# One evacuation put later on ScalarE, one row sum put earlier on VectorE, in a two-block transformer kernel

## The chip, the cores and the metric

The kernel runs on one core of a Trainium2 chip. The metric is the device time of one execution in microseconds (us). The median of three runs before the change is 1176.83 us (1176.0 to 1178.22). The core's engines are named as in the profile: PE is TensorE (PEld its weight loads), DVE is VectorE, ACT is ScalarE, POOL is GpSimd, and SP is SyncE, which issues most DMAs. Each engine runs its own instructions strictly in the order in which they were written; semaphores order the engines among each other.

## The reference, cut to what matters

```python
def project(h, w_in, w_dec_up, b_dec):            # first block; h is 256 x 1024, once for x and once for ctx
    z = h @ w_in
    q, k, v, g, dd, cb, cc, ch, ga, gb = jnp.split(z, ...)
    zd = dd @ w_dec_up + b_dec
    log_a = jax.nn.log_sigmoid(zd) / DECAY_TAU     # decays of the gated linear attention, both directions
...
mod_lat = jnp.split(jax.nn.silu(c) @ w_ada + b_ada, 6)   # shifts, scales and gates, a vector of 6 * 1024
pl = project(modulate(rmsnorm(x, g_mix), sh1, sc1), ...)
pc = project(modulate(rmsnorm(ctx, g_mix), sh1c, sc1c), ...)
o_l = gla_bidir(...)                               # attention over x, from the states that ctx leaves
mix_l = merge_branches(o_l, g, cb, cc, ch, ga, gb, ...)  # y_gla and y_conv, gated, merged, projected
x = x + gt1 * mix_l
x = x + gt2 * swiglu(modulate(rmsnorm(x, g_ffn), sh2, sc2), w_ffn_in, w_ffn_out)
return second_block(rmsnorm(x, g_final), ...)      # feed forward, attention, feed forward
```

## The kernel before, in words

Everything is float32. A product is made of three passes: each weight and each activation is held as a rounded high part (`whi`, `A_hi`, `B_hi`) and the remainder (`wlo`, `A_lo`, `B_lo`), and PE does high by high, high by low and low by high.

The first block's projections are cut into 45 **units** (the list `P1`), each 256 columns wide: unit 0 is `dd`, 1 and 2 are `k`, 3 to 6 are `v`, 7 and 8 are `q`, 9 to 20 are `cb`, `cc`, `ch` four times over, 21 to 24 are `g`, 25 to 28 `conv_out`, and so on. `U_K` is 1, `U_V` is 3, `U_Q` is 7, `U_CB` is 9. A unit's weights come by one DMA of 1 MB into one of three `raw` buffers, ACT writes `whi` (the first half of `split(u)`), DVE subtracts to get `wlo` (the second half, which also gives the buffer free for the load of unit u + 3), and PE runs the unit. The units `k` and `v` are computed for `x` and for `ctx` and take two banks of PSUM each: unit 2 has banks 4 and 7, unit 3 banks 5 and 6, unit 4 banks 4 and 7, unit 5 banks 5 and 6. All later units have one bank, 4 and 5 by turns. Before it starts unit u, PE waits until its `lo_ready` has come and until the unit that last held its banks has been **evacuated** (`wait_banks`): for `v` ACT does this with two copies, for `ch` DVE does it with a multiplication by `cc` (two units later PE uses that bank again).

ACT and DVE each walk through the same loop over u. In its round u, ACT evacuates unit u - 1 (`evac1(u - 1)`), does its half of `split(u + 2)`, and then what the attention needs at that point (`gla_front`, `gla_step`), the `ch` convolution's middle tap (`conv_tap`) and its high part. The exceptions stand at the start: at u = `U_K + 1` unit 2 is evacuated inside `gla_front`, between the exponentials `decays(0)`, `decays(1)` and the part `log_decays(2)`; at u = `U_V` unit 3 is evacuated inside `gla_front` ahead of `decays(2)` and `decays(3)`. The `decays(g)` wait for DVE's running sums of the decays, `sums(g)` (semaphores `scan_done` and `d_done`).

`decays(2)` and `decays(3)` have to be done before DVE can form the decayed keys (`decayed_keys`), which PE turns after half of unit 6 (`turn_keys`).

The modulation vector of `w_ada` is made beside the units, 256 columns at a time (numbers 0 to 15 in this part). POOL issues the 1 MB load of number n into the one buffer `ada_raw` when number n - 1 is through (`load_ada`). DVE's `adapt(n)` waits for the landing and folds the eight 128 x 256 pieces into a row of sums, eight instructions one after the other. The table `MOD_STEP` says at the end of which round u DVE does which `adapt(n)`.

At u = 21 DVE's round is: evacuate unit 20 (`ch`, the fourth), `split(23)`, `conv(3)` with four taps and a product, `adapt(8)`. At u = 20 it has only `split(22)`.

Of the kernel before, what the change touches and what calls it, by code (L numbers as in the profile page):

```python
# [54 lines left out]
U_K, U_V, U_Q, U_CB = (P1.index((s, 0)) for s in ("k", "v", "q", "cb"))  # L55
# [62 lines left out]
ADA_LAST = ADA_P2 + NADA2  # L118


MOD_STEP = {4: 0, 5: 1, 7: 2, 9: 3, 11: 4, 13: 5, 16: 6, 18: 7, 21: 8, 24: 9, 26: 10, 28: 11, 30: 12, 32: 13, 34: 14, 36: 15}

ADA_FFN = [n for n in range(len(ADA)) if NADA1 <= n < ADA_P2 or n >= ADA_LAST]
ADA_MIX = [n for n in range(len(ADA)) if n not in ADA_FFN]
ADA_DVE = [n for n in range(len(ADA)) if n in MOD_STEP.values() or n in ADA_FFN or ADA_P2 <= n < ADA_P2 + 4]
ADA_POOL = [n for n in range(len(ADA)) if n not in ADA_DVE]
# [22 lines left out]
def build(nc, a, out):  # L149
    with ExitStack() as ctx:  # L150
# [711 lines left out]
        def _(act):  # L862
# [7 lines left out]
            def run(o, i, f=ACT.Copy, **kw):  # L870
                return nc.scalar.activation(o, i, f, **kw)  # L871

            def split(u, i=0, count=1):

                if isinstance(i, int) and u + 3 * i >= UNITS:
                    return
                act.wait_ge(landed[ring(u)], landings(u, i))
                if not isinstance(i, int) or u + 3 * i >= RING:
                    act.wait_ge(unit_used, lin(3, i, u - RING + 1))
                run(whi[ring(u)][:], raw[ring(u)][:]).then_inc(hi_ready, count)  # L880
# [66 lines left out]
            def conv_high(n):  # L947
                act.wait_ge(v_done, n + 1)
                run(B_hi[:, 2 * n:2 * n + 2, :], uS.rearrange("p (m t) -> p m t", m=2)).then_inc(vhi_done, 1)

            def evac1(u):
                kind, n = P1[u]
                eng, count = EV1[u]
                b = BANKS1[u]
                act.wait_ge(unit_used, u + 1)
                two = slice(2 * n, 2 * n + 2)
                b3 = [bank[x][:].rearrange("p (m t) -> p m t", m=2) for x in b]
                if kind == "dd":
                    run(dd_out, bank[0][:, 0:P]).then_inc(act_evac, 1)
                elif kind == "k":  # L960
                    run(kT1[:, two, :], b3[0])
                    run(kTc[:, two, :], b3[1]).then_inc(act_evac, 1)
                elif kind == "v":
                    run(v_l[:, :, UC * n:UC * n + UC], b3[0])
                    run(v_c[:, :, UC * n:UC * n + UC], b3[1]).then_inc(act_evac, 1)
                elif kind == "q":
                    run(qT1[:, two, :], b3[0], scale=float(HK) ** -0.5).then_inc(act_evac, 1)
                elif kind in ("cb", "cc"):
                    if n >= 2:
                        act.wait_ge(v_done, n - 1)  # L970
                    run((cbS if kind == "cb" else ccS)[n % 2], bank[b[0]][:]).then_inc(act_evac, 1)
                elif kind == "conv_out":
                    run(yT[:, two, :], b3[0]).then_inc(act_evac, 1)
                elif kind == "g":
                    if n:
                        act.wait_ge(dve_evac, EV1[u - 1][1])
                    run(T0, bank[b[0]][:], ACT.Sigmoid).then_inc(sig_done, 1)
                elif kind in ("ga", "gb"):
                    run((siga if kind == "ga" else sigb)[:, two, :], b3[0], ACT.Sigmoid).then_inc(act_evac, 1)
                    if kind == "ga":  # L980
                        act.wait_ge(ont_tr, n + 1)
                        run(B_hi[:, two, :], bank[6 + n % 2][:].rearrange("p (m t) -> p m t", m=2))\
                            .then_inc(onhi_done, 1)
                elif kind == "gla_out":
                    act.wait_ge(mg_done, n + 1)
                    run(A_hi[:, two, :], (T0, T1)[n % 2].rearrange("p (m t) -> p m t", m=2)).then_inc(mghi_done, 1)

            def conv_tap(n):

                act.wait_ge(dve_evac, EV1[P1.index(("ch", n))][1])  # L990
                for m in range(2):
                    c = VEC["w_conv"] + KD + 2 * n + m
                    ins = run(yS[:, T * m:T * m + T], uS[:, T * m:T * m + T], scale=vec[:, c:c + 1])
                ins.then_inc(tap_done, 1)

            def log_decays(g0):

                act.wait_ge(zd_mm, 2 * g0 + 4)
                for s in range(2):
                    for g in (g0, g0 + 1):  # L1000
                        d, p, order = gla_pass(g)
                        E = pair3(Eb[g] if s == 0 else Lb[g])
                        for h in range(2):
                            col = VEC["b_dec"] + H1 * d + 2 * p + h
                            ins = run(token_halves(E[:, h, :]), decay_part(g, s, h), ACT.Abs, bias=vec[:, col:col + 1])
                        ins.then_inc(z_abs, 1)

            def soft_part(g):

                act.wait_ge(z_abs, 2 * g + 4)  # L1010
                for v in (Eb[g], Lb[g], Eb[g + 1], Lb[g + 1]):
                    ins = run(v, v, ACT.Exp, scale=-1.0)
                link(ins)
                for v in (Eb[g], Lb[g], Eb[g + 1], Lb[g + 1]):
                    run(v, v, ACT.Ln, bias=1.0).then_inc(z_log, 1)

            def decays(g):

                d = g // 2
                act.wait_ge(scan_done, g + 1)  # L1020
                R, E = pair3(Mc[g % 2]), pair3(Eb[g])
                lo, hi = slice(0, T - 1), slice(1, T)
                run(E[:, :, lo] if d == 0 else E[:, :, hi], R[:, :, hi] if d == 0 else R[:, :, lo], ACT.Exp,
                    scale=1.0 / 16).then_inc(ex_done, 1)
                act.wait_ge(d_done, g + 1)
                run(alpha[:, g], alpha[:, g], ACT.Exp, scale=1.0 / 16)
                run(Qb[g], Ml[g % 2], ACT.Exp, scale=1.0 / 16)
                run(Lb[g], Ml[g % 2], ACT.Exp, scale=-1.0 / 16).then_inc(eq_done, 1)

            def key_tokens(g):  # L1030

                act.wait_ge(kt_tr, g + 1)
                run(k_tok[g].rearrange("p a b c -> p (a b c)"), bank[g][:]).then_inc(kt_sb, 1)

            def ctx_key_tokens(g):

                act.wait_ge(ktc_tr, g + 1)
                run(Eb[g], bank[g][:]).then_inc(ktc_sb, 1)
# [12 lines left out]
            def gla_front(u):  # L1051

                if u == U_K:
                    log_decays(0)
                    soft_part(0)
                if u == U_K + 1:
                    decays(0)
                    decays(1)
                    evac1(U_K + 1)
                    log_decays(2)  # L1060
                    soft_part(2)
                if u == U_V:
                    evac1(U_V)
                    decays(2)
                    decays(3)
                if u == U_V + 3:
                    for g in range(4):
                        ctx_key_tokens(g)
                if u == U_Q:
                    for g in range(4):  # L1070
                        key_tokens(g)

            def gla_step(slot):

                if slot in (2, 3, 4):
                    scale_state(0, slot - 2)
                    scale_state(1, slot - 2)
                if slot in (9, 10, 11):
                    scale_state(2, slot - 9)
                    scale_state(3, slot - 9)  # L1080
# [175 lines left out]
            split(2)  # L1256

            for u in range(N1):
                if u and u not in (U_V, U_V + 1):
                    evac1(u - 1)  # L1260
                if u:
                    split(u + 2)
                gla_front(u)
                gla_step(2 * (u - 1 - U_Q) + 1)
                if P1[u - 1][0] == "ch":
                    conv_tap(P1[u - 1][1])
                if P1[u - 2][0] == "ch":
                    conv_high(P1[u - 2][1])
                gla_step(2 * (u - U_Q))
                if u == U_CB + 7:  # L1270
                    head_squares()
# [621 lines left out]
        def _(dve):  # L1893
# [626 lines left out]
            for u in range(N1):  # L2520
# [14 lines left out]
                if u == U_CB + 8:  # L2535
                    norm_heads()
                if u in MOD_STEP:
                    n = MOD_STEP[u]
                    adapt(n, 0, acc[:, UC * ada_pos(n):UC * ada_pos(n) + UC], ADA[n][0])
# [60 lines left out]
```

## Time and profile before

| | |
|---|---|
| median of the runs | 1176.83 us |
| the profiled execution's own time | 1176.83 us |
| its span in the profile | 1174.9 us |
| PE busy, DVE busy, ACT busy | 96%, 73%, 48% of the span |
| mean granted clock of PE | 0.978 of full speed |

The span is counted from the first to the last instruction that the profile shows; the profiled execution's own time is 1.9 us more. PE's busy time is modelled at the ends of matmuls, so a busy PE is not one at its peak; what can be read safely is when a matmul starts and how long PE sat idle before it. A row of the timeline gives the start, the duration of the merged group, the engine, the line, the operation and its tiles, the count, and in brackets the idle time before it with what ended it. Almost all instructions of one engine stand on the line of a helper, so tiles and times tell which one it is.

### The profile page before, as it was taken

How to read it: one execution, taken by the hardware profiler on the slowest of the kernel's cores; microseconds unless marked ns; L12 is line 12 of the kernel's file. 1: busy time of each engine (PE TensorE's matmuls, PEld its weight loads, DVE VectorE, ACT ScalarE, POOL GpSimd, SP SyncE). 2: the span in 40 equal slices, each digit the busy share in tenths (PEclk: the TensorE clock that was granted, in tenths of full speed). 3: DMA queues.
4: the chain of work that ended last, by engine and by line, in shares of the span. 5: the costliest groups of instructions: out<-in, count | busy, mean ns of one | idle time of the engine just before them, and what ended most of it. 6: DMA issues, size and time to landing. Idle time of an engine off the chain costs nothing.

```text
span 1174.9 us, 19118 instructions
## 1 busy us (share of the span) xinstructions
PE 1130.0 (96%) x7764; PEld 1025.0 (87%) x7764; DVE 857.3 (73%) x1072; ACT 569.7 (48%) x729; POOL 146.4 (12%) x162
## 2 busy tenths in 40 slices
PE   2999999999999999999899999999999989999996
PEld 2999988999999888888788888899989989888885
DVE  2678766897877787787877887778655796755676
ACT  3595433544433544444545444455655536444442
POOL 4000000100001000000200000020476561000000
PEclk8999999999999999999899999989999989999999
DMA  9924654688866487787468877647744745655770
GB/s 288 310 84 144 208 163 139 200 285 278 289 203 211 164 272 250 261 265 272 160 198 272 263 238 252 224 145 260 251 147 153 238 144 170 227 195 181 234 246 36
DMA packets 192548, 250.28 MB, mean 213 GB/s; under 512 B 4860, under 2 KB 171967, under 8 KB 192351
## 3 DMA queue, kind: packets, MB, share of 16 engines
q1 hardware_dynamic: 183838, 216.92, 56.7%
q0 software_dynamic: 8640, 32.38, 8.2%
q8 instruction: 51, 0.84, 0.3%
q14 instruction: 19, 0.15, 0.0%
HBM read 248.23 MB, written 1.05 MB: 212 GB/s over the span
## 4 chain that ended last, share of the span: by engine, by line
PE 87%; DVE 7%; issue 2%; SPq 2%; ACT 1%; DMA 1%; POOL 0%; POOLq 0%; DVEq 0%; ACTq 0%
PE twin L1296 84%; DVE wlo L1902 2%; DVE arena L1910 2%; DVE arena L1902 2%; PE twin L1357 1%; DMA arena<-in_w_ada 1%; ACT arena L871 1%; ACT whi L871 0%; DVE X L1902 0%; PE twin L1622 0%; SPq L564 0%; SPq L514 0%; PE twin L1739 0%; PE twin L1410 0%; DVE B_lo L1902 0%
## 5 line engine op out<-in xcount | busy, mean ns | idle before, releaser
L1296 PE MATMUL twin<-A_both,whi 128*128 128x256 f32 (+1 forms) x2208 | 579.9, 339 | 1.2 <-DVE arena L1902 1.1
L1902 DVE TENSOR_TENSOR wlo<-raw,whi 128x2048 fp32r<-128x2048 f32 x169 | 397.4, 2352 | 121.3 <-ACT whi L871 121.2
L1296 PE MATMUL twin<-A_both,wlo 128*128 128x256 f32 x1632 | 436.7, 280 | 0.0
L871 ACT ACTIVATE whi<-raw 128x2048 fp32r<-128x2048 f32 x169 | 323.1, 1912 | 207.8 <-PE twin L1296 206.6
L1296 PEld LDWEIGHTS twin<-A_both,whi 128*128 128x128 f32 x2208 | 371.5, 190 | 43.6 <-issue 6.2
L1296 PEld LDWEIGHTS twin<-A_both,wlo 128*128 128x128 f32 x1632 | 309.8, 190 | 11.1 <-DVE A_both L1902 0.2
L1910 DVE SCALAR_TENSOR_TENSOR arena<-ada_raw,arena 128x256 f32<-128x256 f32 (+1 forms) x308 | 149.4, 485 | 11.0
L871 ACT ACTIVATE arena<-twin 128x512 f32<-128x512 f32 (+5 forms) x167 | 88.5, 555 | 114.9 <-PE twin L1296 85.5
L871 ACT ACTIVATE arena<-arena 128x512 f32<-128x512 f32 (+7 forms) x132 | 69.8, 558 | 150.1 <-DVE arena L1902 114.4
L1296 PE MATMUL twin<-whi,B_hi 128*128 128x512 f32 (+2 forms) x340 | 126.6, 372 | 0.2 <-DVE B_lo L1902 0.2
L1296 PE MATMUL twin<-wlo,B_hi 128*128 128x512 f32 (+2 forms) x340 | 125.1, 368 | 0.0
L1296 PE MATMUL twin<-whi,B_lo 128*128 128x512 f32 (+2 forms) x340 | 125.1, 368 | 0.0
L1296 PE MATMUL twin<-whi,A_both 128*128 128x256 f32 x640 | 118.8, 288 | 4.6 <-DVE A_both L1902 4.6
L1902 DVE TENSOR_TENSOR arena<-arena,twin 128x512 f32<-128x512 f32 x92 | 62.6, 685 | 64.4 <-ACT arena L871 50.1
L1296 PEld LDWEIGHTS twin<-whi,A_both 128*128 128x128 f32 x640 | 101.5, 195 | 5.9 <-issue 5.8
L1296 PE MATMUL twin<-wlo,A_both 128*128 128x256 f32 x320 | 91.3, 285 | 0.0
L1296 PE MATMUL twin<-arena 128*128 128x1 f32 (+10 forms) x656 | 80.9, 296 | 0.1
L1296 PEld LDWEIGHTS twin<-whi,B_lo 128*128 128x128 f32 x340 | 64.1, 189 | 11.3 <-issue 0.7
L1296 PEld LDWEIGHTS twin<-wlo,B_hi 128*128 128x128 f32 x340 | 64.1, 188 | 10.7
L1296 PEld LDWEIGHTS twin<-arena 128*128 128x128 f32 (+5 forms) x656 | 66.6, 174 | 7.8 <-DVE arena L2225 0.3
L1296 PEld LDWEIGHTS twin<-whi,B_hi 128*128 128x128 f32 x340 | 64.1, 189 | 10.2 <-issue 1.1
L1296 PE MATMUL twin<-B_hi,whi 128*128 128x256 f32 x224 | 63.9, 285 | 1.9 <-DVE B_lo L1902 1.1
(134 smaller groups left out, 986.4 us busy)
## 6 DMA issues: line engine op xcount, KB each, us to landing
raw<-in_w_in SPq DMA_DIRECT2D x48, 1024.0 KB, 5.7
raw<-in_ffn_w_in SPq DMA_DIRECT2D x44, 1024.0 KB, 5.1
ada_raw<-in_w_ada POOLq DMA_DIRECT2D x28, 1024.0 KB, 6.5
ada_raw<-in_w_ada SPq DMA_DIRECT2D x24, 1024.0 KB, 5.4
raw<-in_w_ffn_in SPq DMA_DIRECT2D x22, 1024.0 KB, 5.1
raw<-in_ffn_w_out SPq DMA_DIRECT2D x22, 1024.0 KB, 4.9
raw<-in_w_ffn_out SPq DMA_DIRECT2D x11, 1024.0 KB, 5.1
arena<-in_w_ada SPq DMA_DIRECT2D x8, 1024.0 KB, 11.8
```

The lines of the kernel that those rows point to most:

```text
L871: return nc.scalar.activation(o, i, f, **kw)
L1296: return nc.tensor.matmul(o, l, r, start=start, stop=stop, **kw)
L1357: ins = nc.tensor.transpose(bank[norm_bank(n, b)][:, c:c + P], src[:, t, P * k:P * k + P], ident)
L1902: return nc.vector.tensor_tensor(o, x, y, op)
L1910: return nc.vector.scalar_tensor_tensor(out=o, in0=x, scalar=sc, in1=y, op0=op0, op1=op1)
```

## The change

Two things move; nothing is added or taken away.

```diff
-MOD_STEP = {4: 0, 5: 1, 7: 2, 9: 3, 11: 4, 13: 5, 16: 6, 18: 7, 21: 8, 24: 9, ...}
+MOD_STEP = {4: 0, 5: 1, 7: 2, 9: 3, 11: 4, 13: 5, 16: 6, 18: 7, 20: 8, 24: 9, ...}
...
                 if u == U_V:
-                    evac1(U_V)
                     decays(2)
                     decays(3)
...
             for u in range(N1):
-                if u and u not in (U_V, U_V + 1):
+                if u and u != U_K + 2:
                     evac1(u - 1)
```

`U_K + 2` is 3, the same round as `U_V`, so in round 3 nothing is different but the evacuation that was taken out of `gla_front`. In round 4 the ordinary `evac1(3)` now runs.

ACT, rounds 3 and 4 of the loop, before. The copies from `twin2` and `twin3` are an evacuation (banks 5 and 6, then 4 and 7), `whi2<-raw2` is `split(5)`, `whi0<-raw0` is `split(6)`, the rows that wait for `scan_done` begin `decays(2)` and `decays(3)`.

```order
L871 ACTIVATE whi2<-raw2 128x2048 [waits unit_used,landed2]
L871 ACTIVATE arena<-twin2 128x2x256 [waits unit_used]
L871 ACTIVATE arena<-twin3 128x2x256
L871 ACT_TABLE_LOAD
L871 ACTIVATE arena<-arena 128x2x255 [waits scan_done]
L871 ACTIVATE arena<-arena 128x8 [waits d_done]
L871 ACTIVATE arena<-arena 128x512 x2
L871 ACTIVATE arena<-arena 128x2x255 [waits scan_done]
L871 ACTIVATE arena<-arena 128x8 [waits d_done]
L871 ACTIVATE arena<-arena 128x512 x2
L871 ACTIVATE whi0<-raw0 128x2048 [waits unit_used,landed0]
```

The same stretch of ACT in the changed kernel:

```order
L871 ACTIVATE whi2<-raw2 128x2048 [waits unit_used,landed2]
L871 ACT_TABLE_LOAD
L871 ACTIVATE arena<-arena 128x2x255 [waits scan_done]
L871 ACTIVATE arena<-arena 128x8 [waits d_done]
L871 ACTIVATE arena<-arena 128x512 x2
L871 ACTIVATE arena<-arena 128x2x255 [waits scan_done]
L871 ACTIVATE arena<-arena 128x8 [waits d_done]
L871 ACTIVATE arena<-arena 128x512 x2
L871 ACTIVATE arena<-twin2 128x2x256 [waits unit_used]
L871 ACTIVATE arena<-twin3 128x2x256
L871 ACTIVATE whi0<-raw0 128x2048 [waits unit_used,landed0]
```

The two copies of unit 3 have moved from ahead of eight instructions of the decays, four of which wait for DVE, to behind them.

DVE, rounds 20 and 21, before. `wlo1` is `split(22)`, `X<-arena,twin2` is the evacuation of unit 20, `wlo2` is `split(23)`, the rows on `X` are `conv(3)`, the two rows on `ada_raw` are `adapt(8)`, and the last one begins the evacuation of unit 21.

```order
L1902 TENSOR_TENSOR wlo1<-raw1,whi1 128x2048 [waits hi_ready]
L1902 TENSOR_TENSOR X<-arena,twin2 128x512 [waits vlo_done,act_evac,unit_used]
L1902 TENSOR_TENSOR wlo2<-raw2,whi2 128x2048 [waits hi_ready]
L1910 SCALAR_TENSOR_TENSOR X<-X,arena 128x4x63 [waits tap_done]
L1910 SCALAR_TENSOR_TENSOR X<-X,arena 128x4x63
L1910 SCALAR_TENSOR_TENSOR X<-X,arena 128x4x63 [waits dve_chain]
L1910 SCALAR_TENSOR_TENSOR X<-X,arena 128x4x63
L1902 TENSOR_TENSOR X<-arena,X 128x512 [waits dve_chain]
L1906 TENSOR_SCALAR arena<-ada_raw,arena 128x256 [waits ada_landed_p]
L1910 SCALAR_TENSOR_TENSOR arena<-ada_raw,arena 128x256 [waits ada_mac] x7
L1902 TENSOR_TENSOR arena<-arena,twin2 128x512 [waits sig_done]
```

The same stretch of DVE in the changed kernel (its line numbers are one lower):

```order
L1901 TENSOR_TENSOR wlo1<-raw1,whi1 128x2048 [waits hi_ready]
L1905 TENSOR_SCALAR arena<-ada_raw,arena 128x256 [waits ada_landed_p]
L1909 SCALAR_TENSOR_TENSOR arena<-ada_raw,arena 128x256 [waits ada_mac] x7
L1901 TENSOR_TENSOR X<-arena,twin2 128x512 [waits vlo_done,act_evac,unit_used]
L1901 TENSOR_TENSOR wlo2<-raw2,whi2 128x2048 [waits hi_ready]
L1909 SCALAR_TENSOR_TENSOR X<-X,arena 128x4x63 [waits tap_done]
L1909 SCALAR_TENSOR_TENSOR X<-X,arena 128x4x63
L1909 SCALAR_TENSOR_TENSOR X<-X,arena 128x4x63 [waits dve_chain]
L1909 SCALAR_TENSOR_TENSOR X<-X,arena 128x4x63
L1901 TENSOR_TENSOR X<-arena,X 128x512 [waits dve_chain]
L1901 TENSOR_TENSOR arena<-arena,twin2 128x512 [waits sig_done]
```

The eight instructions of `adapt(8)`, the first of which waits for a DMA, have moved from behind the evacuation of unit 20, `split(23)` and `conv(3)` to ahead of them. PE, POOL and SP have the same instructions in the same order as before.

## Rows read from the trace of the kernel before

**Rows 1.** The page: busy time of PE over the span.
```profile
PE 1130.0 (96%) x7764; PEld 1025.0 (87%) x7764; DVE 857.3 (73%) x1072; ACT 569.7 (48%) x729; POOL 146.4 (12%) x162
```

**Rows 2.** The page: chain that ended last, shares of the span by engine.
```profile
PE 87%; DVE 7%; issue 2%; SPq 2%; ACT 1%; DMA 1%; POOL 0%; POOLq 0%; DVEq 0%; ACTq 0%
```

**Rows 3.** Busy time by stretches: us, busy PE, PEld, DVE, ACT, POOL, PEclk, DMA.
```profile
91.00:97.00 6.00, 6.00 (x52) 6.00 (x51) 5.90 (x14) 3.16 (x5) 0.00 (x0) 1.00 0.56 172
```

**Rows 4.** Timeline of PE: the first matmuls of units 4 and 5.
```profile
79.24 0.40 PE L1296 MATMUL twin<-whi,A_both 128*128 128x256 f32 x2
...
90.76 0.40 PE L1296 MATMUL twin<-whi,A_both 128*128 128x256 f32 x2
```

**Rows 5.** Timeline of ACT, 84 to 98 us: evacuation, decays, `split(6)`.
```profile
85.81 1.06 ACT L871 ACTIVATE arena<-twin 128x512 f32<-128x512 f32 x2
...
91.63 0.63 ACT L871 ACTIVATE arena<-arena 128x510 f32<-128x510 f32 x1 [1.68 <-DVE arena L2158]
94.47 1.25 ACT L871 ACTIVATE arena<-arena 128x8 f32<-128x8 f32 x3 [2.21 <-DVE arena L1902]
95.63 1.90 ACT L871 ACTIVATE whi<-raw 128x2048 fp32r<-128x2048 f32 x1
```

**Rows 6.** Timelines: DVE's last decayed key; PE's first turning of keys.
```profile
98.84 0.68 DVE L1902 TENSOR_TENSOR arena<-arena 128x512 f32<-128x512 f32 x1
...
108.04 1.91 PE L1410 MATMUL twin<-arena 128*128 128x128 f32 x16
```

**Rows 7.** PE around its longest idle time in a run of units.
```profile
947.09 0.77 PE L1296 MATMUL twin<-whi,A_both 128*128 128x256 f32 x2 [4.56 <-DVE A_both L1902]
...
951.57 0.40 PE L1296 MATMUL twin<-whi,A_both 128*128 128x256 f32 x2
```

**Rows 8.** Busy time by stretches, around the same place.
```profile
944.50:947.00 2.50, 0.00 (x0) 0.00 (x0) 2.50 (x3) 0.00 (x0) 2.20 (x2) 0.51 0.02 5
...
949.00:951.00 2.00, 2.00 (x11) 2.00 (x11) 1.87 (x4) 1.36 (x3) 0.00 (x0) 0.50 1.14 365
```

**Rows 9.** Timeline of PE around two shorter idle times.
```profile
878.77 0.63 PE L1622 MATMUL twin<-arena 128*128 128x128 f32 x4 [1.75 <-ACT arena L871]
...
880.37 0.77 PE L1296 MATMUL twin<-A_both,whi 128*128 128x256 f32 x2
...
883.07 0.43 PE L1296 MATMUL twin<-A_both,whi 128*128 128x256 f32 x2
...
915.37 0.36 PE L1296 MATMUL twin<-B_hi,whi 128*128 128x256 f32 x1 [0.84 <-ACT arena L871]
```

**Rows 10.** Timeline of DVE, 233 to 247 us.
```profile
233.15 2.29 DVE L1902 TENSOR_TENSOR wlo<-raw,whi 128x2048 fp32r<-128x2048 f32 x1
235.53 0.69 DVE L1902 TENSOR_TENSOR X<-arena,twin 128x512 f32<-128x512 f32 x1
...
239.77 1.78 DVE L1910 SCALAR_TENSOR_TENSOR X<-X,arena 128x252 f32<-128x252 f32 x4
...
242.19 0.35 DVE L1906 TENSOR_SCALAR arena<-ada_raw,arena 128x256 f32<-128x256 f32 x1
...
246.10 0.68 DVE L1902 TENSOR_TENSOR arena<-arena,twin 128x512 f32<-128x512 f32 x1
```

**Rows 11.** POOL's issue of load 8; its landing; the landings of eight such loads.
```profile
230.73 0.88 POOL L773 DMA_DIRECT2D ada_raw<-in_w_ada  x1 [13.51 <-DVE arena L1910]
...
DMA to landing us min/median/max: 8.0/8.0/8.0
...
DMA to landing us min/median/max: 6.0/7.0/8.0
```

**Rows 12.** Timeline of PE: the first matmuls of units 22 and 23.
```profile
241.09 0.40 PE L1296 MATMUL twin<-whi,A_both 128*128 128x256 f32 x2
...
246.93 0.47 PE L1296 MATMUL twin<-whi,A_both 128*128 128x256 f32 x2
```

**Rows 13.** Timeline of ACT: tap of `conv(3)`, table load for the sigmoid.
```profile
237.43 0.89 ACT L871 ACTIVATE X<-X,arena 128x256 f32<-128x256 f32 x2
238.34 1.28 ACT L871 ACT_TABLE_LOAD   x1
```

More of the change, by code:

```diff
@@ L118 @@
 ADA_LAST = ADA_P2 + NADA2
-MOD_STEP = {4: 0, 5: 1, 7: 2, 9: 3, 11: 4, 13: 5, 16: 6, 18: 7, 21: 8, 24: 9, 26: 10, 28: 11, 30: 12, 32: 13, 34: 14, 36: 15}
+MOD_STEP = {4: 0, 5: 1, 7: 2, 9: 3, 11: 4, 13: 5, 16: 6, 18: 7, 20: 8, 24: 9, 26: 10, 28: 11, 30: 12, 32: 13, 34: 14, 36: 15}
 ADA_FFN = [n for n in range(len(ADA)) if NADA1 <= n < ADA_P2 or n >= ADA_LAST]
```

## The prediction

> **What bounds the kernel now.** I read the page first: PE is busy for 96% of the span [rows 1], and the chain that ended last runs through PE for 87% of it [rows 2]. So this kernel takes as long as PE's queue, and an edit on ACT or DVE matters only where it makes PE start a matmul later or earlier. The busy times by stretches say the same of the first place that the change touches: from 91 to 97 us PE is busy for 6.00 of 6.00 us at the full clock [rows 3], with no slack in it. The reader is to look in the timelines at the start of each unit on PE, and to ask for each which evacuation and which `wlo` it had to have by then.
>
> **Part one: the evacuation of unit 3 on ACT.** Unit 5 goes into banks 5 and 6, which unit 3 held, so PE can't start it before unit 3's two copies are done. Units 4 and 5 start at 79.24 and 90.76 us [rows 4], 11.52 us for 96 matmuls, or 0.12 us each, back to back. Before the change the two copies are at 85.81 and take 1.06 us [rows 5]: done at 86.87, 3.9 us ahead of need.
>
> After the change they stand behind `decays(2)` and `decays(3)`. When does ACT get through these? In the trace it waits twice there for DVE: until 91.63 for the scan of `sums(3)` and until 94.47 for the last differences, and the three exponentials behind that take it to 95.63, where `split(6)` starts [rows 5]. Taking the copies out in front gives ACT 1.06 us, but all of it is lost in those waits, since DVE sets both and doesn't depend on the copies. So the copies start at 95.63 and end at 96.69. How long does PE take to wake? The evacuation of unit 21 on DVE ends at 246.10 + 0.68 = 246.78 [rows 10] and unit 23 in the same bank starts at 246.93 [rows 12]: 0.15 us. Unit 5 starts at 96.84 and not at 90.76: **6.1 us** of PE standing still. There is no deadlock in it, because sums and decays of both directions have their PE inputs already. I know no reason that would move this by more than 0.3 us either way, as every duration is a row of the same place.
>
> What is queued behind the copies on ACT is `split(6)`, now at 96.6 to 98.5. DVE's half of it comes after the last decayed key, 98.84 + 0.68 [rows 6], so it is not late, and unit 6 needs it only at 96.84 + 11.52 = 108.4. Unit 4's evacuation, next on ACT, is due at that time too. Nothing there costs more.
>
> Can the 6.1 us be won back later? PE turns the keys at 108.04, and the decayed keys were ready at 99.5 [rows 6]: 8.5 us of slack that grow, which is worth nothing, because PE did not wait for them. From here to the feed forward DVE, ACT and the loads follow PE's units, so they move along with it. I count all of it.
>
> **The clock behind that stop.** The trace has a like case: PE stood still for 4.56 us until 947.09 [rows 7]; the granted clock was 0.51 in the stretch before it started again and 0.50 from 949 to 951 [rows 8], that is the lower of the two levels (1.2 GHz). From 947.09 to 951.57 [rows 7] lie 21 matmuls, 4.48 us; at 0.12 each they are 2.52. Lost: **2.0 us**. The stop in question is longer, so I take the same. Both ends: below, nothing, which is what the stop of 0.84 us at 915.37 [rows 9] shows, where the matmuls went on at full pace; above, the low level lasted from 944.5 to 951.1 in that case, 6.6 us, and if PE worked all that time it would lose half, 3.3 us. The page "TensorE: Matmul & The Clock Gate" of the Trainium skill (section "HAM oscillation — how this bites in real kernels") says that a wait for data between two bursts makes the next one start at half rate; the row at 947.09 agrees with it.
>
> **Part two: `adapt(8)` one round earlier on DVE.** Before, `split(22)` ends at 235.4, and the evacuation of unit 20 follows at 235.53; `adapt(8)` runs from 242.19 to 246.10, 3.91 us [rows 10]. Now it stands directly behind `split(22)`. Its data: POOL issues the load at 230.73, as soon as `adapt(7)` is through (that does not change), and this load took 8.0 us to land [rows 11], so it lands at 238.73. DVE waits there for 3.3 us with four things queued behind it: the evacuation of unit 20, `split(23)`, `conv(3)` and the evacuation of unit 21. `adapt(8)` ends at 238.73 + 3.91 = 242.64, the evacuation of unit 20 at + 0.68 = 243.32, PE + 0.15 = 243.47. Unit 22, which takes unit 20's bank, started at 241.09 [rows 12]. That is **2.4 us** more. Times here are those of before; by then everything stands some 8 us later, DVE, POOL and PE alike, since DVE had waited for PE between the two places.
>
> Bounds: eight such loads landed in 6.0 to 8.0 us [rows 11]. With 6.0 the stop is 0.4 us; if a landing is counted from the end of the issue (0.88 us) and not from its start, it is 3.3. I take 2.4, as this very load took 8.0. The page "DMA: Bandwidth & Descriptors" of the Trainium skill (section "Issuing engines are not separate DMA queues") says that loads issued by POOL and by SP share the same 16 engines and interleave; by that rule the landing depends on the weight loads beside it, whose order is as before, and the sum stays with the 8.0 of the row.
>
> What is late next? Unit 23 needs the evacuation of unit 21. In the trace it comes just in time (246.78 for a start at 246.93). Now DVE does the evacuation of unit 20 (0.69), a `split` (2.29, as at 233.15) and `conv(3)` (239.77 to 242.19, 2.42) behind `adapt(8)` [rows 10]: 5.4 us without a wait, from 242.64 to 248.0, and the evacuation of 21 ends at 248.7. ACT's tap, table load and sigmoid ahead of it come behind the evacuation of unit 20 too; at 0.89 and 1.28 us for the first two [rows 13] and 0.6 for the sigmoid they are through at 246.2, earlier than DVE. Unit 23 would start at 243.47 + 5.76 (48 matmuls) = 249.2. It is in time by 0.4 us, and `split(24)` and the later rounds have more, since `adapt(8)` isn't in their way any more. So part two costs its one stop. What it gives, load 9 issued 3.5 us earlier, nobody waits for.
>
> **The sum.** 6.1 + 2.0 + 2.4 = 10.5 us. The profiled execution took 1176.83 us with a span of 1174.9, 1.9 us around it, and is itself the median of the runs, so 1176.8 + 10.5 = **1187.3 us**, 0.9% slower.
>
> **Rivals.**
> - *The clock falls a second time*, behind the stop at unit 22. For it: after the stop of 1.75 us at 878.77 the matmuls from 880.37 to 883.07, four steps of three, took 2.70 us in place of 1.44 [rows 9]; 1.3 us lost. Against it: there PE had been thinly used for some time, while here it is full on both sides. It gives 1188.6. [...]
> - *Only the first stop is there*: load 8 lands in about 6 us, and unit 22 starts 0.4 us late. For it: the median of eight such loads is 7.0 us and the fastest took 6.0 [rows 11]. Against it: the one at this place took 8.0. It gives 1176.8 + 6.1 + 2.0 + 0.4 = 1185.3.
> - *The clock stays up in both*: 1176.8 + 6.1 + 2.4 = 1185.3. Against it stands the row at 947.09.
> - *Not slower*: the bank of unit 5 is not what holds PE. If PE came to unit 5 only at 96.8 us or later, the copies would be hidden, and ACT would hand over the exponentials of `decays(2)` 1.06 us earlier, which could bring the decayed keys forward. That decides from the point where PE runs 6.1 us behind ACT's queue; it gives at best 1176.8 - 1.1 = 1175.7, if the keys were waited for. Against it: PE was at unit 5 at 90.76 and idle nowhere before it, and the keys had 8.5 us to spare.
>
> **How the numbers follow.** The forecast with both stops and one fall of the clock has a chance of 0.52; the clock falling twice 0.16; only the first stop 0.15; no fall 0.12; not slower 0.05. The range is to hold 8 in 10: its low end is the cases near 1185.3 less 2 us, for a landing and a clock that both come out kind, 1183; its high end is 1188.6 with 1 us for a longer low clock (the bound of 3.3 and not 2.0) and half a microsecond for the spread of the runs, 1190. Differences under 0.2% (2.4 us) can't be told from no change; all cases but the last are slower by 8 us and more, so slower has 0.95, within 0.2% 0.03, faster 0.02.
>
> **What the profile after would show.** Right: ACT's pair of copies from `twin` at about 95.6 us; PE idle for about 6 us ahead of a `whi,A_both` matmul near 96.8, released by ACT; a stretch behind it at clock 0.5; DVE idle for about 3 us ahead of an `ada_raw` row some 8 us later than 235.4, released by a DMA; PE idle for about 2 us ahead of unit 22, released by DVE. Wrong: no idle time on PE before 100 us; or PE idle in both places and the span no longer, which would mean that PE waited somewhere later for something that does not move with it.

## The result, and the profile after

The changed kernel takes 1190.29 us (median, 1188.13 to 1195.96) against 1177.53 us before (1176.0 to 1179.31): the ratio is 1.0111 with an interval of [1.0083, 1.0139]. It is slower by 12.8 us where 10.5 were forecast. 1190.29 lies just above the range, which ended at 1190. The profiled execution took 1189.37 us, with a span of 1187.6 us.

ACT of the changed kernel between 84 and 99 us, to be held against [rows 5]. The columns are those of the timelines ahead of the prediction.

```profile
87.60 1.77 ACT L871 ACTIVATE arena<-arena 128x510 f32<-128x510 f32 x4
92.01 0.63 ACT L871 ACTIVATE arena<-arena 128x510 f32<-128x510 f32 x1 [2.64 <-DVE arena L2157]
94.85 1.25 ACT L871 ACTIVATE arena<-arena 128x8 f32<-128x8 f32 x3 [2.21 <-DVE arena L1901]
96.00 1.07 ACT L871 ACTIVATE arena<-twin 128x512 f32<-128x512 f32 x2
```

ACT starts `decays(2)` earlier and loses it all in a longer wait for DVE (2.64 in place of 1.68 us). The copies of unit 3 come at 96.00. Everything in this execution stood 0.37 us later from the start on (the `x3` row at 94.85, before at 94.47), so this is the 95.63 of the working.

PE of the changed kernel, same view: unit 5 starts, the keys are turned, unit 22 starts, and the first rows of `on` are turned behind unit 29.

```profile
97.22 0.77 PE L1295 MATMUL twin<-whi,A_both 128*128 128x256 f32 x2 [5.90 <-ACT arena L871]
...
116.63 1.91 PE L1409 MATMUL twin<-arena 128*128 128x128 f32 x16
...
252.05 0.71 PE L1295 MATMUL twin<-whi,A_both 128*128 128x256 f32 x2 [2.22 <-DVE X L1901]
...
299.69 0.60 PE L1879 MATMUL twin<-arena 128*128 128x128 f32 x4
```

These are two new idle times of PE, each released by the evacuation that was moved or blocked. The same last row before the change:

```profile
287.32 0.60 PE L1880 MATMUL twin<-arena 128*128 128x128 f32 x4
```

From such starts each price can be taken, without the modelled ends. Between unit 5 and the turned keys lay 108.04 - 90.76 = 17.28 us [rows 4, 6]; now it is 116.63 - 97.22 = 19.41, so 2.13 us are lost behind the first stop. Between unit 22 and the turned rows lay 287.32 - 241.09 = 46.23 us [rows 12]; now it is 47.64: 1.41 us are lost behind the second. The granted clock is in the busy times by stretches of the changed kernel (us, busy PE, PEld, DVE, ACT, POOL, then PEclk, DMA share, GB/s):

```profile
97.20:99.20 2.00, 1.99 (x9) 2.00 (x10) 2.00 (x6) 2.00 (x2) 0.00 (x0) 0.50 0.00 0
99.20:101.20 2.00, 2.00 (x12) 2.00 (x11) 2.00 (x4) 2.00 (x3) 0.00 (x0) 0.50 0.00 0
...
102.50:105.00 2.50, 2.50 (x24) 2.50 (x23) 2.33 (x5) 0.00 (x0) 0.00 (x0) 1.00 0.64 141
...
252.00:254.00 2.00, 1.95 (x9) 1.98 (x10) 2.00 (x1) 1.98 (x3) 0.50 (x1) 0.53 0.63 205
...
256.00:258.00 2.00, 2.00 (x19) 2.00 (x18) 1.97 (x4) 1.19 (x2) 0.00 (x0) 1.00 0.91 307
```

In both places the granted clock fell to the lower of the two levels: PE worked about 4.7 us at half pace behind the first stop and 3.4 behind the second.

DVE of the changed kernel around `adapt(8)`, to be held against [rows 10]:

```profile
241.73 2.28 DVE L1901 TENSOR_TENSOR wlo<-raw,whi 128x2048 fp32r<-128x2048 f32 x1
247.31 0.35 DVE L1905 TENSOR_SCALAR arena<-ada_raw,arena 128x256 f32<-128x256 f32 x1 [3.29 <-DMA ada_raw<-in_w_ada]
...
251.22 0.68 DVE L1901 TENSOR_TENSOR X<-arena,twin 128x512 f32<-128x512 f32 x1
...
256.44 0.68 DVE L1901 TENSOR_TENSOR arena<-arena,twin 128x512 f32<-128x512 f32 x1
```

DVE waits 3.29 us for the landing, as worked out, and hands over the bank of unit 20 after it. The evacuation of unit 21 ends at 257.12, and unit 23 starts without idle time: that cover held. POOL had issued the load at 239.31; it took 8.0 us again.

### The profile page after: what moved, and what is told of

Same layout as the page of the kernel before. It is cut to its first block, busy times and chain, and to the rows that moved or that the text cites. A ratio compares the mean times of both kernels' runs of the same rounds, so it can differ in the third digit from the quotient of the medians.

```text
span 1187.6 us, 19118 instructions
## 1 busy us (share of the span) xinstructions
PE 1135.0 (96%) x7764; PEld 1030.1 (87%) x7764; DVE 857.5 (72%) x1072; ACT 569.7 (48%) x729; POOL 149.1 (13%) x162
## 4 chain that ended last, share of the span: by engine, by line
PE 81%; DVE 11%; ACT 3%; issue 2%; DMA 2%; SPq 2%; POOL 0%; POOLq 0%; DVEq 0%; ACTq 0%
PE twin L1295 78%; DVE wlo L1901 3%; DVE arena L1909 3%; DVE arena L1901 3%; ACT arena L871 2%; PE twin L1356 1%; DMA arena<-in_w_ada 1%; DMA ada_raw<-in_w_ada 1%; ACT whi L871 1%; DVE X L1901 1%; PE twin L1621 0%; SPq L514 0%; SPq L564 0%; DVE B_lo L1901 0%; ACT L871 0%
## 5 line engine op out<-in xcount | busy, mean ns | idle before, releaser
L1295 PE MATMUL twin<-whi,A_both 128*128 128x256 f32 x640 | 122.4, 293 | 12.8 <-ACT arena L871 5.9
L1295 PEld LDWEIGHTS twin<-whi,A_both 128*128 128x128 f32 x640 | 104.2, 200 | 14.3 <-issue 9.4
```

The source lines that it names most:

```text
L1295: return nc.tensor.matmul(o, l, r, start=start, stop=stop, **kw)
```

## The experiments

All are ratios to the kernel before, on a shared chip. The kernel before itself ran from 1171.9 to 1184.3 us beside them, median near 1178.2, so that ratios have intervals of 0.15 to 0.3%, which is 1.8 to 3.5 us. Effects of 1 or 2 us are therefore read from the traces, one execution each, and not from the times.

**e1_act_only**: the ScalarE part alone.

```diff
                 if u == U_V:
-                    evac1(U_V)
                     decays(2)
...
-                if u and u not in (U_V, U_V + 1):
+                if u and u != U_K + 2:
```

> Only the evacuation of unit 3 on ScalarE is moved behind decays(2) and decays(3); adapt(8) stays in round 21. Theory (two bank waits on TensorE, each with its own fall of the clock): TensorE stands still 5.9 us ahead of unit 5 and loses 2.0 us of clock behind it, nothing at unit 22: 7.9 us slower than before, about 1185, ratio 1.0067. Rival (the two moves cost more together than apart, for example because everything behind unit 5 is already late when adapt(8) comes): under 6 us or over 10 us. Rival (the clock behind the stop is a matter of chance, not of the stop): 5.9 us, 1183.

Measured 1.0068 [1.0043, 1.0092], 8.0 us. PE in its trace:

```profile
97.91 0.77 PE L1295 MATMUL twin<-whi,A_both 128*128 128x256 f32 x2 [5.91 <-ACT arena L871]
...
116.50 1.91 PE L1409 MATMUL twin<-arena 128*128 128x128 f32 x16
...
295.78 0.60 PE L1879 MATMUL twin<-arena 128*128 128x128 f32 x4
```

The stop is there at full length, none is at unit 22, and 18.59 - 17.28 = 1.31 us of clock were lost here. The two parts add up within their intervals: 8.0 for this one and 3.4 for the next are 11.4, and both together gave 13.1 and 12.4 by their ratios.

**e2_dve_only**: the VectorE part alone. **e10_dve_look** is one more execution of the same kernel.

```diff
-MOD_STEP = {..., 18: 7, 21: 8, ...}
+MOD_STEP = {..., 18: 7, 20: 8, ...}
```

> Only adapt(8) is moved to round 20 on VectorE; the evacuation of unit 3 stays where it was. Theory: VectorE waits 3.3 us for load 8, TensorE stands still 2.2 to 2.5 us ahead of unit 22 and the clock falls once behind it, 1.3 us: 3.8 us slower, about 1181, ratio 1.0032. If the clock stays up in most runs: 2.4 us slower, about 1179.5. Rival (the second stop exists only because of the first): no idle time of TensorE at unit 22 and no difference, 1177.

> The kernel of e2_dve_only once more, for one look: does the clock fall behind the stop ahead of unit 22? It fell in both traces of the changed kernel and in neither of the two traces with the VectorE move alone (stops of 3.0 and 2.0 us). Theory (a stop of 2 to 3 us between full stretches lies on the edge, so that it falls in some executions): either may be seen. Rival (it falls only where the first stop is there too): no fall again.

Measured 1.0029 [1.0009, 1.0048], 3.4 us. PE in the two traces, e2 and then e10:

```profile
109.20 1.91 PE L1410 MATMUL twin<-arena 128*128 128x128 f32 x16
...
245.44 0.47 PE L1296 MATMUL twin<-whi,A_both 128*128 128x256 f32 x2 [3.03 <-DVE X L1902]
...
291.58 0.60 PE L1880 MATMUL twin<-arena 128*128 128x128 f32 x4
```

```profile
245.95 0.47 PE L1296 MATMUL twin<-whi,A_both 128*128 128x256 f32 x2 [2.31 <-DVE X L1902]
...
292.10 0.60 PE L1880 MATMUL twin<-arena 128*128 128x128 f32 x4
```

The second stop does not need the first. From unit 22 to the turned rows are 46.14 and 46.15 us, as before the change: the fall of the clock that I had expected here, 1.3 us, came in neither trace, though both stops are longer than the 2.22 us that was followed by a fall. Load 8 took 8.8 us in e2 and 8.1 in e10, and the length of the stop follows it.

**e4_between**: `adapt(8)` in round 20, and unit 3's evacuation between the two decays.

```diff
                 if u == U_V:
-                    evac1(U_V)
                     decays(2)
+                    evac1(U_V)
                     decays(3)
```

> adapt(8) in round 20 as in the changed kernel, but the evacuation of unit 3 stands between decays(2) and decays(3) on ScalarE. Theory (only the need of unit 5 at 90.8 us counts, the place before or behind decays(2) does not): ScalarE reaches it at about 89 us, in one of its waits for VectorE, done at 90.1, so no stop at unit 5; the time is that of the kernel with the VectorE move alone, about 1181. Rival (any delay of this evacuation, or a finer dependence on the decays, costs): a stop of TensorE ahead of unit 5, over 1182.

Measured 1.0014 [0.9997, 1.0031], not told from the kernel before. ACT in its trace:

```profile
89.62 1.06 ACT L871 ACTIVATE arena<-twin 128x512 f32<-128x512 f32 x2
92.34 0.63 ACT L871 ACTIVATE arena<-arena 128x510 f32<-128x510 f32 x1 [1.66 <-DVE arena L2158]
```

The copies end at 90.68, just inside what unit 5 needs; PE had no idle time there and stood still only at unit 22 (2.02 us, landing 7.8 us, no fall). So it is not the place behind `decays(2)` that costs, but copies that end later than unit 5 wants its banks.

**e3_warm_both**: the changed kernel with the waits of PE filled. The matmuls of ones go into bank 3, and nobody reads them.

```diff
                 pe.wait_ge(lo_ready, u + 1)
+                if u == U_V + 2:
+                    pe.wait_ge(z_abs, 8)
+                    pe.wait_ge(z_min, 8)
+                    keep_warm(3, 48)
+                if u == U_CB + 13:
+                    pe.wait_ge(on_done, 8)
+                    keep_warm(3, 18)
                 wait_banks(u, BEFORE1[u], EV1)
```

> The changed kernel, with 48 matmuls of ones into a free bank ahead of the bank wait of unit 5 (about 5.3 us) and 18 ahead of that of unit 22 (about 2.0 us); their results are used by nobody. Theory (stop and clock are two separate prices): the stops stay as long, 5.9 and 2.2 us, but the clock stays at its upper level behind both, so 3.4 us less than the changed kernel: about 1187, 8.5 us over before. Rival (the slow matmuls behind a stop are not due to the idle engine): same time as the changed kernel, 1190, with clock 0.5 still there. If 48 or 18 matmuls take longer than the waits, the time is above 1187 by the overshoot.

Measured 1.0135 [1.0105, 1.0165]: a miss of mine in the size. One such float32 matmul shows as two instructions, so 48 of them took 10.88 us and overshot the wait. The clock did stay up (17.36 us from unit 5 to the turned keys, as before the change), but the time could not show it.

**e5_warm_half**: the same with 24 and 9.

> The changed kernel with half as many matmuls of ones as in e3_warm_both: 24 ahead of the bank wait of unit 5 and 9 ahead of that of unit 22. One such matmul is two instructions of 0.11 us, so they fill about 5.3 of the 5.9 us and 2.0 of the 2.2 us, and overshoot neither wait. Theory (stop and clock are separate prices): unit 5 starts at about 97.2 us as in the changed kernel, but at the full clock, so units behind it are 2.0 us earlier, and no fall behind unit 22 either (up to 1.4 us there); total over before 8.4 to 9 us, ratio 1.0074. Rival (the slow matmuls come from something else than the idle engine): shift behind unit 5 still grows by 2 us and the time equals that of the changed kernel.

Measured 1.0062 [1.0043, 1.0081], against 1.0105 of the unfilled kernel beside it. PE in its trace:

```profile
91.81 5.52 PE L1295 MATMUL twin<-ones 128*128 128x128 f32 x48
97.77 0.51 PE L1295 MATMUL twin<-whi,A_both 128*128 128x256 f32 x2 [0.43 <-ACT arena L871]
...
115.15 1.91 PE L1409 MATMUL twin<-arena 128*128 128x128 f32 x16
```

Unit 5 had to wait for ACT just as long, but from it to the turned keys are 17.38 us and not 19.41: the clock's price is gone and the stop's is not. Behind unit 22 it is gone too: 46.17 us to the turned rows, where the changed kernel has 47.64. Stop and clock are separate prices, and the clock's follows from PE standing idle. The gain of 5 us in the ratio is more than the 4.3 by which the trace of e5 is shorter in these two places than that of e8, the unfilled kernel beside it; the intervals allow for that.

**e8_after_again** and **e11_after_look** (a single execution): the changed kernel itself.

> The changed kernel again, unaltered, beside the others of this call. Theory: 5.9 us stop, 1.2 to 2.1 us of clock behind it, 2.0 to 3.0 us stop ahead of unit 22 (by the landing of load 8, 7.8 to 8.8 us), and 0 or 1.4 us of clock behind that: 9.1 to 12.4 us over before, ratio 1.008 to 1.0105. Rival (the moves cost something else beyond the two stops): ratio over 1.011 with the two stops as long as in the first trace.

> The changed kernel once more, for one look: theory (the fall at unit 22 is a matter of the execution): either may be seen, with a price of 0 or 1.4 us; behind unit 5 it falls in every execution, with a price of 1.2 to 2.9 us. Rival (tied to the first stop): falls again in both places.

Measured 1.0105 [1.0085, 1.0124], 12.4 us; e11's one execution took 1191.44 us. PE in e8:

```profile
98.05 0.77 PE L1295 MATMUL twin<-whi,A_both 128*128 128x256 f32 x2 [5.88 <-ACT arena L871]
...
118.09 1.91 PE L1409 MATMUL twin<-arena 128*128 128x128 f32 x16
...
253.68 0.47 PE L1295 MATMUL twin<-whi,A_both 128*128 128x256 f32 x2 [2.39 <-DVE X L1901]
...
301.31 0.60 PE L1879 MATMUL twin<-arena 128*128 128x128 f32 x4
```

The clock's price behind unit 5 was 20.04 - 17.28 = 2.76 us here, more than the 1.2 to 2.1 that I had expected, and 2.63 in e11; behind unit 22 it was 1.40 in both. A stop of 2.2 to 2.5 us was thus followed by a fall in three of three traces of the changed kernel, and one of 2.0 to 3.0 us in none of the three traces without the first stop. Its length alone can't be what decides.

The busy times by stretches of e8 show where the lower level begins and ends, around unit 5 and around unit 22:

```profile
97.00:97.50 0.50, 0.00 (x0) 0.00 (x0) 0.50 (x2) 0.50 (x2) 0.00 (x0) 0.87 0.00 0
104.00:104.50 0.50, 0.50 (x5) 0.50 (x5) 0.46 (x2) 0.00 (x0) 0.00 (x0) 0.80 0.68 121
254.00:254.50 0.50, 0.50 (x6) 0.50 (x5) 0.50 (x1) 0.48 (x3) 0.12 (x1) 0.88 0.33 115
257.50:258.00 0.50, 0.50 (x5) 0.50 (x4) 0.50 (x1) 0.50 (x1) 0.00 (x0) 0.71 0.97 389
```

A PEclk between 0.50 and 1.00 says that the level changed within the stretch: it was low from about 97.37 to 104.20 us and from 254.38 to 257.79. Read in the same way, the lower level lasted 6.8 us at the first stop in all four traces that have it (after, e1, e8 and e11), and at the 4.56 us stop before the change. What differs is when it begins: 1.9 us after PE had stopped in e1, 3.8 in the first trace of the changed kernel, 5.2 in e8, 4.9 in e11. That leaves 2.8, 4.7, 6.2 and 5.8 us of it for the time in which PE works again, and a little under half of that is the price: 1.31, 2.13, 2.76 and 2.63. At unit 22 it lasted 3.4 us in all three traces and began only when PE had started again, 0.1 to 0.7 us later.

**e6_evac_first**: `adapt(8)` in round 21, but directly behind the evacuation of unit 20.

```diff
                 if u:
                     evac1(u - 1)
+                if u == 21:
+                    adapt(8, 0, acc[:, UC * ada_pos(8):UC * ada_pos(8) + UC], ADA[8][0])
```

> The kernel before, but adapt(8) on VectorE stands in round 21 between the evacuation of unit 20 and split(23). VectorE waits there for load 8 as in the changed kernel. Theory (the stop is the evacuation queued behind the waiting adapt(8), not the wait itself): no idle time ahead of unit 22; the next thing that comes late is the evacuation of unit 21, behind adapt(8), split(23) and conv(3), so TensorE stands still about 1.3 us ahead of unit 23 (2.1 if load 8 takes 8.8 us): 1.3 us slower, ratio 1.001. Rival (3.3 us of waiting on VectorE cost what they cost wherever they stand): 2.4 us or more, ahead of unit 22 or 23.

Measured 1.0002 [0.9987, 1.0017]. PE in its trace:

```profile
250.54 0.47 PE L1296 MATMUL twin<-whi,A_both 128*128 128x256 f32 x2 [1.34 <-DVE arena L1902]
```

DVE waits 2.77 us for load 8, PE doesn't stop at unit 22, and it stops for 1.34 us at unit 23, as expected; the time can't show so little. A wait on DVE costs what it delays beyond the margin of the next thing that PE needs, and no more.

**e9_bias_later**: e2 with the 512 KB broadcast of the gate's bias issued behind load 9.

```diff
-                if n == 8:
+                if n == 9:
                     pool.wait_ge(on_done, 8)
                     gate_bias(0)
```

> adapt(8) in round 20 on VectorE, evacuation of unit 3 where it was (as e2_dve_only), and the 512 KB broadcast of the gate's bias, which GpSimd issues right behind load 8, is issued behind load 9. Theory (the stop ahead of unit 22 is the landing of load 8, and the landing is set by what else is in flight): load 8 lands in about 7 us and not in 7.8 to 8.8, VectorE waits about 1 us less, and the stop ahead of unit 22 is 1.2 us and not 2.0 to 3.0: 1.3 us over before, ratio 1.001. Rival (the landing is the same without the broadcast, held up by the two weight loads): stop and ratio as in e2_dve_only, 1.003.

Measured 0.9996 [0.9978, 1.0013]. Its load 8, issued by POOL at 231.59, and DVE and PE behind it:

```profile
DMA to landing us min/median/max: 5.9/5.9/5.9
```

```profile
237.55 0.35 DVE L1906 TENSOR_SCALAR arena<-ada_raw,arena 128x256 f32<-128x256 f32 x1 [1.25 <-DMA ada_raw<-in_w_ada]
...
242.30 0.48 PE L1296 MATMUL twin<-whi,A_both 128*128 128x256 f32 x2 [0.18 <-DVE X L1902]
```

The landing fell by more than I expected, from about 8 to 5.9 us, and the second stop is gone: 0.18 us. Load 9, which the broadcast now follows, took 9.0 us, and nobody waited for it. With the broadcast behind it load 8 took 7.8 to 8.8 us in all thirteen other traces; load 9, without one, took 6.1 to 8.4 there. So the long landing goes with the broadcast, though only one trace has it moved.

**e7_warm_before** and **e12_warm_two**: the kernel before, with its own stops filled.

```diff
                     if (kind, n) == ("out2", 0):
                         gate(3)
+                        keep_warm(0, 19)
...
                 shift_and_scale(n, column_bank(n))
+                if n == 3:                 # e12 alone
+                    keep_warm(6, 12)
```

> The kernel before the change, with 19 matmuls of ones into a free bank behind the gate row of the last projection of the second block's attention part, in TensorE's own stop of 4.6 us ahead of 947.1 us. Theory: they fill 4.2 us of the stop, the clock stays up behind it, and the kernel is 2.0 us faster than before, ratio 0.998. Rival (a filled stop is no gain, since the next wait takes what the clock gives): no difference, the matmuls start at the same time and a later stop grows by 2 us.

> The kernel before the change, with matmuls of ones in two of TensorE's own stops: 19 ahead of 947 us as in e7_warm_before, and 12 (2.6 us) ahead of the turning of the rows for the second feed forward, in the stop of 2.7 us ahead of 577.3 us. Theory (a filled stop keeps the clock up): 2.0 us from the first and 1 to 2.5 us from the second, since the clock is low there from 572.4 to 582.7 us in the trace of before: ratio 0.9965. Rival (the clock comes back no earlier, or what it gives is taken by the next wait): no difference, ratio 1.000, as e7_warm_before measured.

Measured 0.9999 [0.9983, 1.0015] and 0.9989 [0.9970, 1.0008]: neither is told from no change. In e7 the clock stayed up, but PE then waited 0.7 us more for the merge's low part, which follows DVE. In e12 the second filling ran at half pace, because the clock was low already:

```profile
577.70 5.14 PE L1296 MATMUL twin<-ones 128*128 128x128 f32 x24
582.68 1.91 PE L1359 MATMUL twin<-arena 128*128 128x128 f32 x16
```

It took 5.14 us where I had counted 2.6 and made the transposes late. No version of these is shown to beat the kernel before.

## Why the prediction was right and wrong

- **First stop, 6.1 us**: right. Idle times of 5.88 to 5.92 us in four traces, and about 0.16 more, since a matmul's modelled end (0.28) lies behind the next start (0.12). e4 shows that it is the bank's time and nothing else.
- **Clock behind it, 2.0 us**: right in kind, and e5 shows that the idle time is its cause. The size was a bit small: 2.13, 2.76 and 2.63 us in the traces of the changed kernel, 2.5 on the mean, and 1.31 in e1. It was taken from one stop as if it were fixed; it is a little under half of the part of the 6.8 us at the lower level that falls behind the stop, and that part differs between executions of one kernel. The bounds of 0 and 3.3 held.
- **Second stop, 2.4 us**: right: 2.22, 2.39 and 2.47 idle, and 0.16 more. That it follows the landing is shown by e2, e4, e9 and e10 (landings of 8.8, 7.8, 5.9 and 8.1 us, idle 3.03, 2.02, 0.18 and 2.31). The rival with an early landing is out for the changed kernel. What the working missed is what sets the landing: it named the weight loads beside it, and e9 points to the broadcast that POOL issues right behind.
- **Clock behind the second stop**: here the step failed. The sum had 0 for it, and the fall was put among the rivals at 0.16. It was there in three traces of three, at 1.4 us. The reason that I gave against it, that PE is full on both sides of the stop, holds just as well for the first stop, where I had counted the fall. The section of the Trainium skill's page "TensorE: Matmul & The Clock Gate" on HAM oscillation does not settle it: it tells of waits of 3 to 5 us between bursts, longer than this stop, and the traces here go both ways, a fall in the three of the changed kernel and none in e2, e4 and e10.
- **Nothing comes late behind them**: right. Unit 23, `split(6)` and the keys had no idle time. Between the turned keys and the turned rows e1 has 295.78 - 116.50 = 179.28 us, as before.

Put together from the three traces: 6.1 + 2.5 + 2.5 + 1.4 = 12.5 us. Measured, first in the result and then in e8, were 12.8 and 11.9 us between the medians, or 13.1 and 12.4 by the ratios. The forecast of 10.5 lacks 1.4 for the second fall, 0.5 for the first and 0.1 for the second stop. That alone gives 1189.3; the rest to 1190.3 is that the runs of before beside it had a median of 1177.53 and not 1176.83, and the scatter. The range's upper end had been built on the rival's 1188.6 with only 1.4 us added, which is too little where single runs of one kernel differ by several us.

What stays open is why the clock fell behind a stop of 2.2 us and not behind one of 3.0. One rival on record, that it falls there only where the first stop is there too, fits all six traces. So does another: with the first stop everything stands some 8 us later, and the stop's place in time could decide. No run here moves the second stop alone, and none has the first stop filled and the second one not, so the two are not told apart.

## What to carry to other kernels

Where a profile shows one engine full, ask of each moved instruction by which time that engine wants its result, read the two starts, and add the wake-up: here that gave the first stop to a tenth of a us and the second to 0.25. Then price the clock behind each stop as well, by a stop of the same trace, take as its bounds how much of the lower level can fall behind the stop, and leave it out of the likeliest case only with a reason that does not also hold for the stops where it is counted. An instruction that waits for a DMA should stand behind the evacuations and not ahead of them, and if it can't, look at what was issued just behind that DMA.

## What had not been expected of the hardware

Load 8, 1 MB issued by POOL, landed in 7.8 to 8.8 us with a 512 KB broadcast issued right behind it and in 5.9 us without (one trace, e9), although it was the first of the two. The lower level of PE's clock lasted 6.8 us at the stops of 4.6 and 5.9 us and 3.4 us at those of 2.2 to 2.5, in every trace where it came, whatever part of it fell into the stop. A float32 matmul of 128 columns took about 0.23 us at the full clock (48 instructions in 5.52 us, two to a matmul) and 0.43 at the lower one (24 in 5.14).
